# Three norms of a two-block transformer kernel: squares taken beside the linear ahead, chunks gathered on VectorE, two sums on TensorE in place of eight

## The reference, cut to what matters

```python
h_lat = modulate(rms_norm(x, norm_g[layer, 0]), m_lat[0], m_lat[1])
...
x = x + m_lat[2] * y_lat
x = x + m_lat[5] * swiglu(modulate(rms_norm(x, norm_g[layer, 1]), m_lat[3], m_lat[4]),
                          ffn_w_in[layer], ffn_w_out[layer])
...
def rms_norm_2(x, w):
    xf = x.astype(jnp.float32)
    y = xf * lax.rsqrt(jnp.mean(xf * xf, axis=-1, keepdims=True) + EPS)
    return (y * w.astype(jnp.float32)).astype(x.dtype)
```

## Time and profile before

| | |
|---|---|
| timed runs before | 3272.82, 3277.46, 3280.25 us (median 3277.46) |
| profiled execution | 3262.18 us |
| its span in the profile | 3260.4 us |
| mean granted TensorE clock | 0.941 |
| instructions | 38562 |
| DMA | 268.57 MB, mean 82 GB/s |

### The profile page before, as it was taken

One profiled execution on the slowest core, in us unless ns is written; L12 is line 12 of the kernel. 1 busy time (PEld: TensorE's weight loads), 2 busy tenths in 40 slices (PEclk: granted clock), 3 DMA queues, 4 the chain that ended last, 5 costly groups with the idle time before them and its releaser, 6 DMA issues. The chain is left out here.

```text
span 3260.4 us, 38562 instructions
## 1 busy us (share of the span) xinstructions
PE 2928.1 (90%) x15516; PEld 2363.9 (73%) x15516; DVE 1280.6 (39%) x1952; ACT 989.3 (30%) x1478; POOL 991.1 (30%) x478
## 2 busy tenths in 40 slices
PE   2889886679999999889998899999899999999998
PEld 1767775568888887868745777787678777886686
DVE  8466555571163125041016606511253454203523
ACT  2235554123211211422103323222244233325432
POOL 0220221113222222643102333444243443342343
PEclk7989898789999999999998999999899999999899
DMA  5300100321242113422103524332220111121121
GB/s 197 122 26 14 46 27 1 123 97 65 69 144 103 64 66 135 149 78 90 68 10 114 191 102 174 137 108 78 78 69 35 40 39 40 38 92 59 54 89 65
DMA packets 48963, 268.57 MB, mean 82 GB/s; under 512 B 5553, under 2 KB 6833, under 8 KB 28593
## 3 DMA queue, kind: packets, MB, share of 16 engines
q1 hardware_dynamic: 48816, 266.54, 23.5%
HBM read 264.42 MB, written 2.10 MB: 82 GB/s over the span
## 5 line engine op out<-in xcount | busy, mean ns | idle before, releaser
L422 POOL TENSOR_TENSOR shared_w_lo<-stage,shared_w_hi 128x2048 fp32r<-128x2048 f32 (+1 forms) x127 | 552.4, 4350 | 1338.6 <-ACT shared_w_hi L392 1336.0
L563 POOL TENSOR_TENSOR shared_w_lo<-stage,shared_w_hi 128x512 fp32r<-128x512 f32 (+2 forms) x233 | 297.6, 1306 | 625.8 <-ACT shared_w_hi L555 625.8
L392 ACT CAST shared_w_hi<-stage 128x2048 fp32r<-128x2048 f32 (+1 forms) x127 | 224.5, 1768 | 481.8 <-PE f0o_acc L485 135.7
L485 PE MATMUL f0i_acc<-norm_b_lo,shared_w_hi 128*128 128x512 f32 (+1 forms) x672 | 172.2, 338 | 0.0
L485 PE MATMUL f0i_acc<-norm_b_hi,shared_w_hi 128*128 128x512 f32 (+1 forms) x672 | 169.7, 333 | 2.0 <-PEq L369 2.0
L630 PE MATMUL two_acc<-norm_f_hi,shared_w_hi 128*128 128x512 f32 (+1 forms) x312 | 131.8, 422 | 9.1 <-DVE norm_f_lo L736 9.1
L828 DVE TENSOR_TENSOR ffn_hidden<-f0i_acc,ffn_gate 128x512 f32<-128x512 f32 (+1 forms) x44 | 22.5, 553 | 296.1 <-PE f0i_acc L485 288.5
L555 ACT CAST shared_w_hi<-stage 128x1024 fp32r<-128x1024 f32 (+2 forms) x117 | 114.7, 1022 | 70.4 <-PE last_acc L630 43.9
L485 PE MATMUL f1i_acc<-norm_e_hi,shared_w_hi 128*128 128x512 f32 x336 | 130.9, 390 | 2.2 <-PEq L369 1.5
L818 ACT CAST ffn_hi<-ffn_hidden 128x768 f32 (+3 forms) x44 | 32.0, 727 | 331.5 <-DVE ffn_hidden L828 331.5
L485 PE MATMUL f1i_acc<-norm_e_lo,shared_w_hi 128*128 128x512 f32 x336 | 130.7, 389 | 0.0
(11 more groups left out here) (577 smaller groups left out, 6955.3 us busy)
## 6 DMA issues: line engine op xcount, KB each, us to landing
stage<-in_w_f0i SPq DMA_DIRECT2D x22, 1024.0 KB, 4.9
stage<-in_w_f1i SPq DMA_DIRECT2D x22, 1024.0 KB, 4.9
stage<-in_w_rv SPq DMA_DIRECT2D x16, 1024.0 KB, 4.9
mod_slots_a<-in_w_mod SPq DMA_DIRECT2D x24, 512.0 KB, 4.8
stage<-in_w_rqk SPq DMA_DIRECT2D x12, 1024.0 KB, 4.9
mod_slots_f<-in_w_mod SPq DMA_DIRECT2D x24, 512.0 KB, 3.7
mod_slots_e<-in_w_mod SPq DMA_DIRECT2D x24, 512.0 KB, 5.5
stage<-in_w_dqkv SPq DMA_DIRECT2D x12, 1024.0 KB, 4.9
```

Of the source, the lines that this page charges most:

```text
L392: nc.scalar.copy(w_hi[:, slot, 0:size], stage[:, slot, 0:size]).then_inc(hi_ready, 1)
L422: nc.gpsimd.tensor_tensor(w_lo[:, slot, 0:size], stage[:, slot, 0:size], w_hi[:, slot, 0:size].bitcast(F32), ALU.subtract)\
L485: mm = nc.tensor.matmul(out[0:min(P, nt), b, 0:m], w[:, k, unit[1]:unit[1] + min(P, nt)], x[:, k, s:s + m], start=begin, stop=end)
L563: last = nc.gpsimd.tensor_tensor(w_lo[:, index % 2, part], stage[:, index % 2, part], w_hi[:, index % 2, part].bitcast(F32), ALU.subtract)
```

## The change

It has four parts, for norms b, e and f alone.

1. `squares_beside` is new. While eo, ro or f1o1 runs, ACT squares each chunk of x as soon as its residual is done, behind the cast of the next weight tile; DVE adds the squares of chunks 1 to 6 to that of chunk 0, in the place of the later `rstd`. The add of chunk c stands on DVE ahead of the residual of chunk c+1. The square of chunk 7 stays by itself.
2. `norm_split(..., beside=True)` sums two tensors on TensorE, the gathered one and the square of chunk 7.
3. In norms b and e, `round_hi(0, 0)` comes behind the root in place of ahead of the squares (`of_act`, and the condition in `linear`).
4. ro and f1o1 get an empty side work (`BY_TILES`), so their tiles are written out in place of looped. The buffers of squares and `rstd` exist from the linear ahead on; `high` and one `join` of the delta stage lie in norm f's room instead of the other way round.

```diff
-                        if side is not None and "sp_first" in side:
+                        if made and not begun and (made.get("beside") or side is not None and "sp_first" in side):
                             made["act"](act, lambda: round_hi(0, 0))
...
+            sums = 1 if beside else DC
...
-                    for c in range(DC):
+                    for c in range(0 if beside else DC):
...
-                    if behind_squares is not None:
+                    if behind_squares is not None and not beside:
                         behind_squares()
-                    act.wait_ge(S["summed"], done["summed"] + DC)
+                    act.wait_ge(S["summed"], done["summed"] + sums)
                     for b, (s, m, _, _) in enumerate(groups):
                         last = nc.scalar.activation(rstd[:, s:s + m], total[:, b, 0:m], ACT.Sqrt, bias=eps_col,
                                                     scale=1.0 / D)
                     last.then_inc(S["root"], 1)
+                    if behind_squares is not None and beside:
+                        behind_squares()
...
+                    if beside:
+                        pe.wait_ge(S["added"], done["added"] + DC - 2)
+                        for b, (s, m, _, _) in enumerate(groups):
+                            nc.tensor.matmul(total[:, b, 0:m], ones[:], rstd[:, s:s + m], start=True, stop=False)
+                        pe.wait_ge(S["squares"], done["squares"] + DC)
+                        for b, (s, m, _, _) in enumerate(groups):
+                            mm = nc.tensor.matmul(total[:, b, 0:m], ones[:], squares[:, (DC - 1) % 2, s:s + m],
+                                                  start=False, stop=True)
+                        mm.then_inc(S["summed"], 1)
+                    for c in range(0 if beside else DC):
...
+        def squares_beside(x_of, groups, home):
+            squares, rstd = home[0:2]
+            squared, added = norm_done.get("squares", 0), norm_done.get("added", 0)
+
+            def square(act, c):
+                if c >= 3:
+                    act.wait_ge(norm_sem["added"], added + c - 2)
+                for s, m in groups:
+                    to = rstd[:, s:s + m] if c == 0 else squares[:, c % 2, s:s + m]
+                    last = nc.scalar.activation(to, x_of(c, s, m), ACT.Square)
+                last.then_inc(norm_sem["squares"], 1)
+
+            def add(dve, c):
+                if 1 <= c < DC - 1:
+                    dve.wait_ge(norm_sem["squares"], squared + c + 1)
+                    wait(dve, norm_sem["added"], added + c - 1)
+                    nc.vector.tensor_tensor(rstd[:], rstd[:], squares[:, c % 2, :], ALU.add).then_inc(norm_sem["added"], 1)
+
+            def square_units(per_tile):
+                def evac(act, t, j, count, res):
+                    for u in range(per_tile):
+                        act.wait_ge(unit_free, count(u))
+                        square(act, t * per_tile + u)
+                return evac
...
                 for u in range(per_tile):
+                    if sums is not None:
+                        sums["add"](dve, t * per_tile + u - 1)
                     dve.wait_ge(unit_done, count(u))
...
-            linear("eo", m_hi, m_lo, feature_units(ALL), None,
-                   add_residual(ALL, [gates_of(0, 0, 0), gates_of(0, 0, 1)], 2, x_again), mixed_cut,
+            linear("eo", m_hi, m_lo, feature_units(ALL), sums_b["units"](2),
+                   add_residual(ALL, [gates_of(0, 0, 0), gates_of(0, 0, 1)], 2, x_again, sums_b), mixed_cut,
...
-            linear("ro", m_hi, m_lo, [("F", 0, ONLY_LAT)], None, add_residual(ONLY_LAT, [gates_of(1, 0, 0)], 1),
-                   mixed_cut)
+            linear("ro", m_hi, m_lo, [("F", 0, ONLY_LAT)], sums_e["units"](1),
+                   add_residual(ONLY_LAT, [gates_of(1, 0, 0)], 1, None, sums_e), mixed_cut, side=BY_TILES)
```

More of the change, by code:

```diff
@@ L665, in program, with norm_split @@
         SCALES_AHEAD = 4
-        norm_sem = {k: sem("norm_" + k) for k in ("squares", "summed", "root", "rstd", "scaled", "hi", "lo")}
+        norm_sem = {k: sem("norm_" + k) for k in ("squares", "summed", "root", "rstd", "scaled", "hi", "lo", "added")}
         norms = [0]
-        def norm_split(x_of, groups, hi, lo, inputs=(), scales=None, home=None):
+        def norm_split(x_of, groups, hi, lo, inputs=(), scales=None, home=None, beside=False):
             n = norms[0]
@@ L756, in of_dve @@
                     low(DC - 1)
-                return dict(act=of_act, pe=of_pe, dve=of_dve, ready=S["lo"], first=done["lo"])
-            for k, m in (("squares", DC), ("summed", DC), ("root", 1), ("rstd", 1), ("scaled", DC), ("hi", DC),
-                         ("lo", DC)):
+                return dict(act=of_act, pe=of_pe, dve=of_dve, ready=S["lo"], first=done["lo"], beside=beside)
+            for k, m in (("squares", DC), ("summed", sums), ("root", 1), ("rstd", 1), ("scaled", DC), ("hi", DC),
+                         ("lo", DC), ("added", DC - 2 if beside else 0)):
                 norm_done[k] = done[k] + m
@@ L841, in feed_forward, with add_residual @@
                         side = out_side[half](inner) if out_side else None
-                        linear(f"f{layer}o{half}", h_hi, h_lo, [("F", 0, segs)], None, residual, ahead=half == 0,
-                               side=side)
+                        if sums is not None and half == 1:
+                            linear(f"f{layer}o{half}", h_hi, h_lo, [("F", 0, segs)], sums["units"](1), sums["residual"], side=BY_TILES)
+                        else:
+                            linear(f"f{layer}o{half}", h_hi, h_lo, [("F", 0, segs)], None, residual, ahead=half == 0,
+                                   side=side)
             weights.close()
-        def add_residual(segs, gates, per_tile, loaded=None):
+        def add_residual(segs, gates, per_tile, loaded=None, sums=None):
             def evac(dve, t, j, count, res):
@@ L2737, in program @@
         dn.close()
+        last_room.close()
         retired = list(d.values()) + list(dc.values())
```

54 lines of the change are left out of this document (37 added, 17 removed).

## The result

The changed kernel takes 3243.64 us (median of 4 runs, 3238.93 to 3244.55), the kernel before 3275.14 (median of 4, 3272.07 to 3280.25). The ratio is 0.9918, 95% interval 0.9898 to 0.9938, so between 20 and 33 us come off (the two medians alone are 31.5 us apart).

A forecast was written before the change was run, and what follows sets the result against it. TensorE, busy 90%, was taken as the bound, with time to gain only where it waits in norms b, e and f. Gains of 1.8, 5.2 and 6.5 us made 13.5 us less: 3264 us, range 3256 to 3271.

The forecast's parts named there:

- the moved cast: Norms b and e: POOL's take_lo behind the cast holds up the scaling, costing 1.5 us in b, 3.05 in e.
- rival 1: Norms b and e: the scaling isn't blocked, so 18.1 us less, 3259; chance 0.17.
- rival 3: f1i0: modulation slots land late, so norm e gives nothing; total gain 8.3 us, 3269; chance 0.07.
- rival 4: Written-out ro and f1o1: TensorE can't be fed, so slower, 3296 at 2 us lost per tile; chance 0.05.
- rival 2: eo eats more than norm b gives: b -4.7 us, total gain 7.0, 3270; chance 0.14.
- I take f's 2.85: Norms e and f: the two sums left on TensorE were priced at 2.85 us, read from norm f's trace.
- lower bound of 1.8: Norm e: its two sums would take 1.8 us at the pace of the later six, 0.9 each.
- Cost 6.2: eo: adds 5.7 us and waits for squares 3.1, less 2.6 put back from shorter DMA waits; b keeps 3.3.
- Everything behind them waits in order, so a shift of the root is a shift of what follows: Behind norms b, e and f: work waits in order behind the scaling's first products, so it moves with the root.
- 13.5 us: Whole kernel: forecast gain, b 1.8, e 5.2 and f 6.5 us together; chance of a 9 to 17 us gain 0.57.

The follow-up runs named there:

- cast_first: The kernel after with the cast of the first weight tile ahead of the sums again in norms b and e; 3243.3 us, 0.9938 of before.
- before_delay_one: The kernel before with one added square on ScalarE between norm f's eight sums and its root; 3263.5 us, 0.9974 of before.
- layout_only: The kernel after with all three norms made as before and tiles looped, only buffer places new; 3267.8 us, 0.9997 of before.

## Why the prediction was right and wrong

**Right.** Each chain went as it was laid out: the root 6.1 us behind the last residual in b (6.0); the moved cast blocks the scaling by way of POOL (1.2 us in b and 2.7 in e, forecast 1.5 and 3.05), so rival 1 is refuted, and cast_first shows that the place of the cast was the reason; adds of 0.956 us (0.95) with three waits of 1.0 (1.03); no late slot (rival 3), no gap in the written-out ro, 89.1 us in both (rival 4). eo did not eat the gain of norm b (rival 2): b gave 4.4 in the table, 3.8 over all profiles.

**Wrong in size, three terms.** "I take f's 2.85" for the two sums of e and f: they took 2.0, because they were over before the clock fell, while the two that I priced by had met its fall. My lower bound of 1.8 was the better price; it is 0.9 in each norm. "Cost 6.2" for eo: the last residual came 88.1 us behind eo's first product with the old norms (mean of 87.0, 88.7, 88.8) and 92.3 after (92.0, 92.7), so 4.2; with the rest of its chain b gave 4.4 in place of 1.8. Part of that is which executions are compared: against the trace that was read (87.0) eo cost 5.3, and over the nine profiles with the old norm (87.6 on the mean) and nine with the new one and its adds (92.8) it cost 5.2.

**Wrong in kind, and the step that failed.** "Everything behind them waits in order, so a shift of the root is a shift of what follows" costed all behind the norms at nothing: no term of the sum says what the granted clock does to work that only starts earlier. With the three sizes mended the forecast would have stayed in its range; what took the time out of it is this. It gave 9 us: 5.8 in the delta stage, 2.0 in the last linears, 1.0 in f1 and 0.4 at the end. The runs show the first two as an effect of the granted clock, which norm f's change sets off, but which isn't a gain of the change: before_delay_one gets them by adding work, and layout_only loses them with every buffer where after has it. The trace of before showed the stretches of 0.50 there, and nothing in it said which of them depend on when the stage starts.

**The base.** I took 13.5 us off the median though the sum was made against an execution 15 us below it. Mended by its own terms (4.4, 6.3 and 7.4), the sum is 18.1, 3259 from the median that I had; with the 9 us it is 3250, against a measured 3243.6 and 3245.1. The rest is mostly the median of three runs that I started from: 20 more executions of before have a median of 3270.4, and 27 off that is 3243. The chances were also summed low: by the rivals' own numbers 0.57 + 0.17 and half of 0.14 + 0.07 make 0.85 for faster, not 0.80. The 1.0 us in f1 stayed without an explanation, and so did what sets how long the clock is low ahead of eo.

## What to carry to other kernels

Taking work off a serial chain between two linears pays its full length, less what the work costs where it goes, and can be read from the timeline (norm f: 7.5 us off the chain, 7.4 off the stretch). Price what is left at the clock that it will meet, not at that of the longer stretch. A change of a few microseconds ahead of a long stage with small or few-row matmuls can also shift where the clock falls, here for 7 to 10 us either way, so time the kernel with a delay of a microsecond or two, and look at where the clock rises behind the stage's start, before crediting a gain to the edit. Where an engine's work is added beside a linear, let it trail by a tile: an add behind two residuals had no wait, one between them had 1 us.

## What of the hardware was unexpected

- Added work made a kernel faster: one square of 0.63 us (and a table load of 1.28) gave 8.5 us (0.9974, interval 0.9958 to 0.9989).
- A run of eight matmuls with 8 of 128 rows took 3.69 or 4.75 us, TensorE busy throughout; in the longer case the low level came with them and lasted into the full products behind.
- One number read from a trace, the time from the delta stage's first product to the rise of the granted clock, sorts the 20 profiles by the length of the stage: 484 to 485 us at 10.8 to 11.9, 489.5 to 495 at 12.3 to 13.1, 487 at 13.1 to 13.7.
- The same products of 512 and 256 columns in turn, at a granted clock of 1.00, started every 173.4 or 176.6 ns on the mean, by stage and execution; f0i takes 447.9 or 452.8 us by it, 4.9 of the 6.4 us by which two executions of the first feed-forward differ (569.6 and 576.0 us).
- A DVE scalar_tensor_tensor with two SBUF inputs is held up by a POOL subtraction just as a tensor_tensor is: 1.99 us in place of 0.75.
